# Dilated attention reads q, k and v where they lie, and TensorE's attention blocks are written out one by one

## The reference, cut to what matters

```python
DIL_GROUPS = ((128, 1), (512, 4), (2048, 16))      # (window, dilation)

def _dilated_prompt(q, k, v, window, dilation, slopes):
    steps = window // dilation                      # 128 keys
    def to_blocks(a):
        a = a.reshape(b, n_sub, dilation, h, e).transpose(0, 2, 1, 3, 4)
        a = jnp.pad(a, ((0, 0), (0, 0), (0, pad), (0, 0), (0, 0)))
        return a.reshape(b, dilation, n_blk, steps, h, e)
...
    s = jnp.einsum('brnqhe,brnkhe->brnhqk', qb, kb, preferred_element_type=jnp.float32) * (e ** -0.5)
    bias = -slopes[:, None, None] * (dilation * dist).astype(jnp.float32)
    s = jnp.where(valid[:, None], s + bias, -jnp.inf)
    m = jnp.max(s, axis=-1, keepdims=True)
    p = jnp.exp(s - m)
    l = jnp.sum(p, axis=-1, keepdims=True)
    o = jnp.einsum('brnhqk,brnkhe->brnqhe', (p / l).astype(v.dtype), vb, preferred_element_type=jnp.float32)
```

## Time and profile before

| | us |
|---|---|
| three runs | 1912.78, 1900.44, 1904.97 |
| median | 1904.97 |
| the profiled execution | 1913.64 |
| its span, first to last instruction | 1912.0 |
| TensorE busy | 1817.2 |
| VectorE busy | 855.8 |
| ScalarE busy | 531.9 |

### The profile page before, as it was taken

How to read it: one execution, slowest core, us unless ns; L and a number is a source line. 1 busy time by engine, 2 the same in 40 slices (tenths; PEclk the granted TensorE clock), 3 DMA queues, 4 the chain that set the end, 5 groups by cost and what they waited for, 6 DMA issues and landing times.

```text
span 1912.0 us, 33797 instructions
## 1 busy us (share of the span) xinstructions
PE 1817.2 (95%) x13392; PEld 1758.3 (92%) x13392; DVE 855.8 (45%) x1515; ACT 531.9 (28%) x1016; POOL 392.8 (21%) x194
## 2 busy tenths in 40 slices
PE   7999999999989999999999879999999999999995
PEld 7999999999978888888999769999999999999994
DVE  3003346674535667655561354442134441144437
ACT  3123334444312333331220353331112221022211
POOL 2121111111111010111221242222222222222314
PEclk9999999999979999999999889999999999999997
DMA  4111112242535455334451001111111111111111
GB/s 168 44 44 43 41 64 75 83 174 85 209 123 175 153 194 197 131 136 173 172 193 47 22 23 44 44 52 48 44 45 49 50 44 45 44 52 47 49 53 78
DMA packets 68091, 170.04 MB, mean 89 GB/s; under 512 B 9320, under 2 KB 38152, under 8 KB 66704
## 3 DMA queue, kind: packets, MB, share of 16 engines
q1 hardware_dynamic: 67280, 167.81, 25.6%
q10 hardware_dynamic: 720, 0.92, 0.1%
HBM read 138.32 MB, written 57.79 MB: 103 GB/s over the span
## 4 chain that ended last, share of the span: by engine, by line
PE 85%; DVE 9%; DMA 2%; issue 2%; ACT 2%; POOL 1%; POOLq 0%; SPq 0%; DVEq 0%; ACTq 0%
PE U L708 60%; PE U L812 7%; PE U L1167 3%; PE B L708 2%; PE B L798 1%; PE B L773 1%; PE B L975 1%; DMA stage<-in_wu 1%; PE B L998 1%; PE B L790 1%; DVE stats L1925 1%; DVE X L1797 1%; PE B L1115 1%; DVE og L1650 1%; DVE XTh L1714 0%
## 5 line engine op out<-in xcount | busy, mean ns | idle before, releaser
L626 POOL TENSOR_TENSOR wl<-stage,wh 128x1024 fp32r<-128x1024 f32 x127 | 309.7, 2438 | 1131.1 <-ACT wh L1188 1131.1
L708 PE MATMUL U<-xh,wh 128*128 128x344 f32 x1368 | 444.2, 325 | 0.2 <-ACT qkv L1192 0.2
L708 PE MATMUL U<-xl,wh 128*128 128x344 f32 x1368 | 437.8, 320 | 0.0
L708 PE MATMUL U<-xh,wl 128*128 128x344 f32 x1368 | 437.7, 320 | 0.0
L708 PE MATMUL U<-hh,wh 128*128 128x344 f32 x1056 | 338.6, 321 | 4.5 <-POOL hl L679 4.5
L708 PE MATMUL U<-hl,wh 128*128 128x344 f32 x1056 | 338.0, 320 | 0.0
L708 PE MATMUL U<-hh,wl 128*128 128x344 f32 x1056 | 337.3, 319 | 0.0
L708 PEld LDWEIGHTS U<-xh,wh 128*128 128x128 f32 x1368 | 258.0, 189 | 0.8 <-ACT qkv L1192 0.5
L708 PEld LDWEIGHTS U<-xh,wl 128*128 128x128 f32 x1368 | 257.8, 188 | 0.0
L708 PEld LDWEIGHTS U<-xl,wh 128*128 128x128 f32 x1368 | 257.7, 188 | 0.0
L708 PEld LDWEIGHTS U<-hh,wh 128*128 128x128 f32 x1056 | 199.2, 189 | 4.6 <-issue 4.6
(11 more groups left out here) (348 smaller groups left out, 2515.3 us busy)
## 6 DMA issues: line engine op xcount, KB each, us to landing
stage<-in_wu SPq DMA_DIRECT2D x126, 512.0 KB, 3.3
out_shift<-in_cache SPq DMA_DIRECT2D x8, 2046.0 KB
gate_scr<-gth SPq DMA_DIRECT2D x16, 516.0 KB, 3.0
gates<-gate_scr SPq DMA_DIRECT2D x8, 1032.0 KB, 5.0
out_shift<-in_cache SPq DMA_DIRECT2D x8, 1022.0 KB
dn_scr<-thb SPq DMA_DIRECT2D x12, 512.0 KB, 2.6
qkv<-in_xT SPq DMA_DIRECT2D x4, 1032.0 KB, 10.5
kvc<-in_cache SPq DMA_DIRECT2D x4, 1024.0 KB, 8.7
```

Source lines behind the costliest of these rows:

```text
L626: nc.gpsimd.tensor_tensor(wl[:, par, :], stage[:, par, :], wh[:, par, :].bitcast(F32), ALU.subtract).then_inc(w_lo, 1)
L708: ins = nc.tensor.matmul(dst, a[:, par, w], b[:, xk, third(j)], start=first and n == 0 and m == 0, stop=last and n == len(ks) - 1 and m == 2)
```

## The change

Three things change. VectorE's copies of k go for all three groups, and those of q and v for groups 0 and 1; `k_st` is gone, and the matmuls and transposes read `qkv` itself through strided views, k of group 2 among them. The scale 1/8 moves from the copy of q into the instruction that adds the bias. And on TensorE alone the 24 blocks are written out one by one (`every_block`) with constants for addresses and counts; the other engines keep their loops. TensorE now waits for `taken` (the projections that it reads) in place of the staged copies, and in group 2 still for q and v.

```diff
+        def every_block():
+            for b in range(3 * BLOCKS):
+                g, r = b // BLOCKS, b % BLOCKS
+                yield b, b % 2, g, (r // 2, r % 2) if g == 1 else r, (b > 0, r % 2 == 1, False)[g]
+
-        def cols(tiles, g, n):
+        def cols(rows, tile, g, n):
+            src = qkv[rows, tile, 0:SEQ]
             if g == 0:
-                return tiles[:, :, bass.ds(n * P, P)]
-            v = tiles.rearrange("p j (i d) -> p j d i", d=DIL[g][1])
+                return src[:, bass.ds(n * P, P)]
+            v = src.rearrange("p (i d) -> p d i", d=DIL[g][1])
             if g == 1:
-                return v[:, :, bass.ds(n[0], 1), n[1] * P:(n[1] + 1) * P].squeeze(2)
-            return v[:, :, bass.ds(n * 2, 2), :]
+                return v[:, bass.ds(n[0], 1), n[1] * P:(n[1] + 1) * P].squeeze(1)
+            return v[:, bass.ds(n * 2, 2), :]
+
+        def earlier(g, n):
+            return n - 1 if g == 0 else (n[0], 0)
...
-            for b, par, g, n, prev, kind in blocks_of(pe):
+            for b, par, g, n, prev in every_block():
...
-                pe.wait_ge(qk_staged, b + 1)
+                pe.wait_ge(taken, 3 * 6 if g == 0 else ALL_QKV)
                 after(pe, biased, b)
+                if g == 2:
+                    pe.wait_ge(q_staged, b - 2 * BLOCKS + 1)
+                t = GT[g]
...
-                                               q_st[rows, j, :], k_st[rows, (par + part) % 2, j, :],
+                                               q_st[rows, j, :] if g == 2 else cols(rows, t + j, g, n),
+                                               cols(rows, t + 2 + j, g, earlier(g, n) if part else n),
...
-                pe.wait_ge(v_staged, b + 1)
+                if g == 2:
+                    pe.wait_ge(v_staged, b - 2 * BLOCKS + 1)
...
-                    ins = nc.tensor.transpose(B7[:, j * P:(j + 1) * P], v_st[:, j, :], ident)
+                    ins = nc.tensor.transpose(B7[:, j * P:(j + 1) * P], v_st[:, j, :] if g == 2 else cols(slice(0, P), t + 4 + j, g, n),
+                                              ident)
...
-                for dst, tile, scale in ((q_st[:], 0, HD ** -0.5), (k_st[:, par], 2, 1.0)):
-                    ins = nc.vector.tensor_scalar(packed(dst, g), cols(qkv[:, t + tile:t + tile + 2, 0:SEQ], g, n),
-                                                  scale, None, ALU.mult)
-                ins.then_inc(qk_staged, 1)
-                after(dve, v_done, b)
-                nc.vector.tensor_scalar(packed(v_st[:], g), cols(qkv[:, t + 4:t + 6, 0:SEQ], g, n),
-                                        1.0, None, ALU.mult).then_inc(v_staged, 1)
+                if g == 2:
+                    after(dve, s_done, b)
+                    v2 = qkv[:, GT[2]:GT[2] + 6, 0:SEQ].rearrange("p j (i d) -> p j d i", d=DIL[2][1])[:, :, bass.ds(n * 2, 2), :]
+                    wide2 = lambda st: st[:].rearrange("p j (d i) -> p j d i", d=2)
+                    nc.vector.tensor_scalar(wide2(q_st), v2[:, 0:2], 1.0, None, ALU.mult).then_inc(q_staged, 1)
+                    after(dve, v_done, b)
+                    nc.vector.tensor_scalar(wide2(v_st), v2[:, 4:6], 1.0, None, ALU.mult).then_inc(v_staged, 1)
...
-                nc.vector.tensor_tensor(sb[:, :, 0:parts, :], s_all[:, :, 0:parts, :], bias[:, :, 0:parts, :],
-                                        ALU.add).then_inc(biased, 1)
+                nc.vector.scalar_tensor_tensor(sb[:, :, 0:parts, :], s_all[:, :, 0:parts, :], HD ** -0.5,
+                                               bias[:, :, 0:parts, :], ALU.mult, ALU.add).then_inc(biased, 1)
```

More of the change, by code:

```diff
@@ L105, in build @@
             q_st = held(early, "q_st", [P, 2, P])
-            k_st = held(early, "k_st", [P, 2, 2, P])
             v_st = held(early, "v_st", [P, 2, P])
@@ L228, in build @@
         bias_in = sem("bias_in")
-        qk_staged, v_staged = sem("qk_staged"), sem("v_staged")
+        q_staged, v_staged = sem("q_staged"), sem("v_staged")
         s_done, biased, maxed, exped = sem("s_done"), sem("biased"), sem("maxed"), sem("exped")
@@ L338, in blocks_of @@
                 yield b, par, 2, i * 2 + (6 + par), False, "z"
-        def cols(tiles, g, n):
+        def every_block():
[4 more added lines that the diff above has]
+            src = qkv[rows, tile, 0:SEQ]
             if g == 0:
-                return tiles[:, :, bass.ds(n * P, P)]
-            v = tiles.rearrange("p j (i d) -> p j d i", d=DIL[g][1])
+                return src[:, bass.ds(n * P, P)]
+            v = src.rearrange("p (i d) -> p d i", d=DIL[g][1])
             if g == 1:
-                return v[:, :, bass.ds(n[0], 1), n[1] * P:(n[1] + 1) * P].squeeze(2)
-            return v[:, :, bass.ds(n * 2, 2), :]
-        def packed(t, g):
-            return t.rearrange("p j (d i) -> p j d i", d=2) if g == 2 else t
+                return v[:, bass.ds(n[0], 1), n[1] * P:(n[1] + 1) * P].squeeze(1)
+            return v[:, bass.ds(n * 2, 2), :]
+        def earlier(g, n):
+            return n - 1 if g == 0 else (n[0], 0)
         def stored_before(b, par, g, n):
@@ L1545, in _ @@
                 u = b + U_BLK
-                dve.wait_ge(taken, 3 * 6 if g == 0 else ALL_QKV)
-                after(dve, s_done, b)
-                t = GT[g]
-                for dst, tile, scale in ((q_st[:], 0, HD ** -0.5), (k_st[:, par], 2, 1.0)):
-                    ins = nc.vector.tensor_scalar(packed(dst, g), cols(qkv[:, t + tile:t + tile + 2, 0:SEQ], g, n),
-                                                  scale, None, ALU.mult)
-                ins.then_inc(qk_staged, 1)
-                after(dve, v_done, b)
-                nc.vector.tensor_scalar(packed(v_st[:], g), cols(qkv[:, t + 4:t + 6, 0:SEQ], g, n),
-                                        1.0, None, ALU.mult).then_inc(v_staged, 1)
+                if g == 2:
[5 more added lines that the diff above has]
+                    nc.vector.tensor_scalar(wide2(v_st), v2[:, 4:6], 1.0, None, ALU.mult).then_inc(v_staged, 1)
                 dve.wait_ge(s_done, b + 1)
```

## The result

| | us |
|---|---|
| before, six runs | 1907.47 median, 1900.44 to 1912.96 |
| changed, six runs | 1916.41 median, 1913.95 to 1920.84 |
| ratio | 1.0045, 95% interval 1.0026 to 1.0064 |
| profiled execution, its span | 1917.63, 1915.7 |

What follows compares the result with a forecast made beforehand. TensorE, busy for 95% of the span, was taken as the bound. The terms, -0.4 us (wait) and +0.6 us (code), gave +0.2 us on the three-run median of 1904.97, so 1905.2 us, with a range of 1898 to 1917.

Steps and rivals of the forecast that it cites:

- rival A: Strided scores and v transposes, groups 1 and 2, slow on TensorE: +15.5 us per doubling; chance 0.12 to factor 2.2, 0.06 above.
- the main line: Whole kernel: no measurable change, 1905.2 us, with the sum of effects within 3 us; chance 0.70.
- Operands with a stride: TensorE's strided reads in groups 1 and 2, 15.5 us exposed: cost taken as 0, at worst +15.5 us at half pace.
- The copies were hidden: VectorE's staging copies, some 20 us, lie beside TensorE; removing them gains only one 0.4 us wait, placed in block 0.
- The waits for `taken`: TensorE waiting for taken projections instead of staged copies in groups 0 and 1: cost 0.
- The 4.4 us marked issue: Idle before the scores' weight loads, 21 times 0.2 us: gain taken as 0, with 4.4 us as the far end.
- Rival B: Small gaps before the scores and the 0.4 us wait vanish: 4.8 us faster, 1900.2 us; chance 0.07.
- The loops: TensorE's attention loops: their jumps cost nothing visible, so writing the blocks out gains 0.
- The code: Loading ten more written-out blocks on TensorE, some 9 packets: cost 0.6 us, far end 8 us.
- rival C: Every added code load on TensorE is exposed: +8 us, 1913 us; chance 0.05.
- The scale: VectorE's bias addition as scalar_tensor_tensor costs the same as tensor_tensor, 513 ns each, with 0.5 us slack: cost 0.
- Block 8's 0.9 us: TensorE's wait for late exponentials in block 8, behind the bias table's transfer: 0.9 us, expected to stay.

Runs made afterwards that it cites:

- the version of group 0 alone: Kernel before with only group 0 read in place, groups 1 and 2 still copied, TensorE written out, scale in the bias addition: ratio 0.9989 (0.9975 to 1.0002).
- the version with group 1 alone: Changed kernel with k of group 2 copied again, so strided operands remain only in group 1: ratio to the kernel before 1.0050 (1.0029 to 1.0070).
- the one with group 2 alone: Kernel before with group 0 and k of group 2 read in place, group 1 copied, TensorE written out, scale moved: ratio 1.0008 (0.9992 to 1.0023).

## Why the prediction was right and wrong

**The number.** 1905.2 was forecast, 1916.4 measured, 0.6% above, and near the top of the range (1917). Of these 11.2 us, 2.5 are the base: six runs of the kernel before have 1907.47 as their median, not the 1904.97 of three. What happened is rival A, to which I gave 0.12 in its mild form; the line that the median would not move, at 0.70, failed. Within 1%, at 0.91, held. That the measured time lies in the range is no merit of the main line: the upper end stood there for rival A at a factor of 1.8. And 1% was too coarse a bound for what can be told from nothing: the interval of the six and six runs was 0.26% to 0.64%.

**The step that failed** is "I take 0" under *Operands with a stride*. The exposed time was right, 15.5 us; its factor was 1 + 10.8/15.5 = 1.7 and not 1. The argument set VectorE's 1.04 ns an element against TensorE's 1.05 ns a column, and neither number holds. VectorE's copies with a step were measured against its convolution steps, which are another instruction. Its own contiguous copies, those of group 0 in the kernel before, are the like to like:

```profile
L1551 DVE TENSOR_SCALAR k_st<-qkv 128x256 f32 x6 | 1.7, 280 | 0.0
```

With 16 bytes between elements the same copy of 256 elements took 397 ns, and with 64 bytes, in group 2, 381 to 388. So VectorE's rows did show a surcharge of the stride, a factor of 1.4, and no larger one for the wider stride; on 15.5 us that is an estimate of some 6 us where I took 0. The 1.05 ns came from 1.19 - 0.65 us, but the records inside a group follow each other by 0.11 us a pair, 0.87 ns a column, so TensorE was faster than I took it to be. With the step they follow each other by 0.22 us: the pace did halve, which the prediction priced at +15.5 us. It cost 10.8, because some 0.2 us of each group (0.65 - 4 x 0.11, 1.06 - 4 x 0.22) and most of the transposes of v did not grow with it.

The line of the Trainium skill's page "SBUF — State Buffer" spoke against this change and was right for the fp32 scores; I gave it too little weight because it gives no size. The prediction also left out that the same page, in its section "Door 1: The DMA port swizzle", calls a stride of 4 fp32 free; here a step of 4 took 1.09 us against 0.65, so the measurement goes against that sentence.

**The copies were hidden**: held. VectorE's busy time fell by 18.3 us (20 forecast), and it bought 0.4 us. But that wait stood in block 17, not in block 0 as I wrote: the row of the waits gives no place. The timeline of the kernel before has it, at the scores of block 17, whose copies came behind a convolution on VectorE:

```profile
395.61 0.72 PE L773 MATMUL B<-k_st,q_st 64*128 64x128 f32 x8 [0.37 <-DVE k_st L1551]
```

The gain was real; "what is late next is nothing" held there too.

**The waits for `taken`** cost nothing: held. **The 4.4 us marked issue** stayed, 5.0 us now in all 24 blocks, so the wait for the staged copy did not make them. The step from 128-row to 64-row operands or something else that did not change may; no run tells. Rival B fell.

**The loops**: held, twice. Written out they gain 0 (1.0005), and the rule on branches of the Trainium skill's page "Runtime: NRT & Kernel Launch", which it states for a target outside the two pages of code that are held, shows no effect for bodies of two blocks. **The code**: 8 more packets, as reckoned (9), and hidden; rival C fell, and of the 0.6 us I had put in, the stage of the written-out version shows 0.1 (337.4 against 337.3 us).

**The scale**: held. The bias addition kept its times, in groups of the changed kernel:

```profile
L1570 DVE SCALAR_TENSOR_TENSOR sb<-B,bias 128x1024 f32<-128x1024 f32 x11 | 13.5, 1225 | 33.1 <-PE B L781 33.1
L1570 DVE SCALAR_TENSOR_TENSOR sb<-B,bias 128x512 f32<-128x512 f32 x13 | 9.0, 692 | 38.3 <-PE B L781 28.9 <-DMA bias<-in_bias 9.5
```

They were 1226 and 692 ns before. VectorE's idle time in front of it, waiting for the scores, is 33.1 + 28.9 = 62.0 us against 35.4. Part of it is only that VectorE comes earlier: the version of group 0 alone, whose scores are not slower, has 43.1. So the time that VectorE was freed of went into waiting for TensorE.

**Block 8's 0.9 us** should have stayed and is 0.4. It hangs on when the bias table lands, and varies between executions: the version with group 1 alone had no such wait, the one with group 2 alone 1.3 us.

## What to carry to other kernels

A copy that another engine makes beside TensorE is free until TensorE waits for it; taking it away moves the stride onto the engine that has no slack. Before reading in place, look at the bytes between neighbours. In the fp32 scores here a contiguous operand costs nothing, a streamed step of two elements 0.01 us a group and a loaded one 0.06, and from 16 bytes on the group took 1.6 to 2 times as long. Keep the copy where the operand is not contiguous; where it is (group 0), reading in place did no harm, and no gain that the times show.

When no row shows an engine doing a thing, a row of another engine bounds little, and it has to be compared with the same instruction: the copy with a step against the contiguous copy (397 against 280 ns), not against another operation. Price the exposed time at a factor of two and let the sum say whether it matters; here that would have been +15 us (10.8 were measured) for a gain of at most 0.4 us from the copies.

## What the hardware showed that was not expected

- fp32 scores: k with a step of 4, 5, 8 or 16 elements took 1.06 to 1.11 us against 0.65, with 3 0.88, with 2 0.66. Loads of q: 2.17 and 2.21 against 1.19.
- fp32r matmuls of 344 columns took 7.4 us for 24 instead of 3.8 with a streamed step of 2, and about the same (7.04 to 7.50) up to 16.
- VectorE's fp32 copies of 256 elements out of qkv took 280 ns contiguous, 397 with 16 bytes from element to element and 381 to 388 with 64.
- Loaded operands of 128 rows and columns with a step of 4 take 0.23 to 0.24 us, in fp32 and fp32r; transposes bear the same step for 0.01 to 0.035 us more each.
- In the kernel with a step in the loads of block 4's product with v, TensorE's granted clock fell to its lower level of 1.2 GHz for part of a stretch (mean 0.72 over 6 us) right behind those 3.63 us of slow loads, where 24 projection matmuls took 5.37 us instead of 3.82, and was back at 1.00 afterwards; the columns are as in the table of stretches:

```profile
214.00:220.00 6.00, 6.00 (x28) 0.72 0.36 110
220.00:230.00 10.00, 10.00 (x77) 1.00 0.01 2
```

  In the changed kernel, whose slow groups are shorter, it stayed at 1.00 through all blocks. It also stayed there in the version with steps in the projections, whose slow thirds of 5.5 to 7.5 us are longer. So that the slow loads made it fall is not shown; it was seen once.
